# Up projection of a decoder layer on one Trainium2 core: seven block products in place of eight

## The reference, cut to what matters

```python
h = rmsnorm(x, norm_ffn_pre)                  # 512 x 1024
u = h @ w_up                                  # 512 x 5632: 2816 gate and 2816 value columns
u = conv_b + sum(conv_w[j] * shifted(u, j) for j in range(3))    # causal, per column
a, b = split(u, 2)
y = (gelu(a) * b) @ w_down                    # 512 x 1024
x = x + rmsnorm(y, norm_ffn_post)
```

## Time and profile before

| | before |
|---|---|
| median of 3 runs | 630.76 us |
| profiled execution | 631.34 us |
| its span, first to last instruction | 629.5 us |
| PE busy | 619.4 us (98%) |
| DVE busy | 420.6 us (67%) |
| ACT busy | 314.0 us (50%) |
| POOL busy | 98.1 us (16%) |
| mean granted clock of TensorE | 0.998 |

### The profile page before, as it was taken

The page is one execution under the profiler, slowest core; times in us unless marked ns, Lnnn a source line. Parts: engine busy times, 40 slices in busy tenths (PEclk is TensorE's granted clock), DMA queues, the critical chain, the costliest instruction groups (busy, mean ns, idle before and its releaser), DMA issues.

```text
span 629.5 us, 8647 instructions
## 1 busy us (share of the span) xinstructions
PE 619.4 (98%) x3062; PEld 511.7 (81%) x3062; DVE 420.6 (67%) x621; ACT 314.0 (50%) x505; POOL 98.1 (16%) x110
## 2 busy tenths in 40 slices
PE   8999999999999999999999999999999999999996
PEld 7887878778787877899888888888888888888885
DVE  3657449647865876884755556566565668988786
ACT  5557338526735834664533334343333336656661
POOL 4313103112210402420000000000000013532203
PEclk9999999999999999999999999999999999999999
DMA  9834223331512354642433233333323436999923
GB/s 274 239 102 134 67 68 101 100 100 50 150 33 100 121 197 151 199 136 68 133 94 104 74 97 98 100 100 97 103 86 101 166 67 111 188 223 228 232 87 133
DMA packets 91947, 78.90 MB, mean 125 GB/s; under 512 B 2617, under 2 KB 76521, under 8 KB 91922
## 3 DMA queue, kind: packets, MB, share of 16 engines
q1 hardware_dynamic: 84434, 61.79, 32.2%
q0 software_dynamic: 7488, 16.80, 13.2%
HBM read 76.46 MB, written 2.12 MB: 125 GB/s over the span
## 4 chain that ended last, share of the span: by engine, by line
PE 91%; DVE 3%; POOL 2%; DMA 1%; issue 1%; ACT 1%; DVEq 0%; SPq 0%; POOLq 0%; ACTq 0%
PE bank L537 82%; PE bank L679 1%; PE bank L617 1%; DMA gains<-in_norm_mix_pre_dram 1%; PE bank L548 1%; POOL grstd L471 1%; PE bank L668 1%; DVE xs L1326 1%; PE bank L608 1%; PE bank L607 1%; POOL work L475 1%; PE bank L658 1%; PE bank L657 1%; DVE yT L1255 1%; DVE gvar L1295 0%
## 5 line engine op out<-in xcount | busy, mean ns | idle before, releaser
L537 PE MATMUL bank<-hT,ws 128*128 128x512 f32 (+1 forms) x1872 | 410.3, 375 | 0.7 <-DVE work L1304 0.6
L537 PEld LDWEIGHTS bank<-hT,ws 128*128 128x128 f32 x1872 | 328.8, 188 | 61.7 <-issue 2.5
L1208 DVE TENSOR_TENSOR ws<-raw,ws 128x1024 fp32r<-128x1024 f32 x87 | 106.2, 1222 | 7.1 <-ACT ws L894 6.7
L537 PE MATMUL bank<-ws,yT 128*128 128x512 f32 x468 | 109.9, 391 | 0.0
L537 PEld LDWEIGHTS bank<-ws,yT 128*128 128x128 f32 x468 | 87.0, 188 | 18.2 <-issue 0.4
L894 ACT ACTIVATE ws<-raw 128x1024 fp32r<-128x1024 f32 x88 | 92.6, 1054 | 15.6 <-PE bank L537 11.5
L1115 ACT ACTIVATE gains<-bank,conv 128x512 f32<-128x512 f32 x22 | 17.2, 781 | 76.8 <-PE bank L537 76.8
L1470 DVE SCALAR_TENSOR_TENSOR gains<-bank,conv,gains 128x511 f32<-128x511 f32 x22 | 16.5, 750 | 53.8 <-ACT gains L1115 53.8
L520 POOL DMA_DIRECT2D late<-in_w_down_dram x8 | 10.7, 1335 | 253.2 <-DVE ws L1510 253.2
L1115 ACT ACTIVATE rot<-bank,conv 128x512 f32<-128x512 f32 x22 | 17.2, 780 | 63.7 <-PE bank L537 63.7
L537 PE MATMUL bank<-ws,hT 128*128 128x512 f32 x186 | 42.8, 389 | 0.0
(11 more groups left out here) (135 smaller groups left out, 597.4 us busy)
## 6 DMA issues: line engine op xcount, KB each, us to landing
raw<-in_w_up_dram SPq DMA_DIRECT2D x44, 512.0 KB, 3.8
raw<-in_w_in_dram SPq DMA_DIRECT2D x28, 512.0 KB, 4.4
raw<-in_w_out_dram SPq DMA_DIRECT2D x16, 512.0 KB, 3.5
raw<-in_w_down_dram POOLq DMA_DIRECT2D x12, 512.0 KB, 7.7
raw<-in_w_down_dram SPq DMA_DIRECT2D x9, 512.0 KB, 4.0
late<-in_w_down_dram POOLq DMA_DIRECT2D x8, 512.0 KB, 5.9
xs<-in_x_dram SPq DMA_DIRECT2D x6, 512.0 KB, 4.1
late<-in_w_down_dram SPq DMA_DIRECT2D x6, 512.0 KB, 6.9
```

The source lines that it names most:

```text
L537: return nc.tensor.matmul(dst, st, mv, start=start, stop=stop, skip_group_check=onto)
L1208: nc.vector.tensor_tensor(ws[:, c, 1, :], raw[:, c, :], f32(ws[:, c, 0, :]), ALU.subtract).then_inc(w_lo, 1)
```

## The change

Sweeps 0 and 1 stay as they are ("plain"). From sweep 2 on, the two value tiles and two gate tiles of a sweep (256 columns each) by the two halves of D, and the two halves of D by the two halves of the tokens, are a 2x2 by 2x2 block product, computed with seven products of sums of blocks. A product is 2 (tiles of 128 weight columns) x 4 (tiles of D) x 3 matmuls, each with 256 tokens. Products accumulate where they can onto each other in PSUM; the others are copied away by ACT and added by DVE.

- Weights: products 1, 4 and 2 take blocks of w_up as SP loads them. Products 7, 6 and 3 take sums laid on product 1's block one after another by POOL's adding transfers, product 5 one on product 4's. A block is 128 partitions x 4 rows of 256 floats, that is 512 KB in pieces of 1 KB; the down projection's are in pieces of 2 KB, and the old w_up loads were in pieces of 512 bytes.
- Activations: `block_sums` (DVE) makes four sums of blocks of h from a float32 copy that ACT keeps (`h_keep`) and from PSUM; `blocks_hi`, `blocks_lo` split them into `yT`.
- Order: one sweep's seven products lie over 16 places of the unit order, so three sweeps are under way at once. In the steady part the order is 1(i), 3(i-2), 4(i-1), 6(i-1), 2(i), 7(i), 5(i-1). The plain units of sweep 1 stand between the first products, and two down units between the last.
- Results: gate in PSUM banks `x_pair(i)` (three pairs), one product in `y_bank(i)`; the value rows go through `vneg`, which lies over `gains[:, 1]`, so the load of `norm_ffn_post` moves from POOL's queue to SP's, behind the last value tap. The taps of the value columns of block sweeps are stored negated, by three copies in place of one.
- Splits run four units ahead in both loops; PSUM banks and the slots of f's shares are laid out anew, and shares follow `shares_at` in place of a fixed distance of six.

```diff
+UP_WHEN = {1: 0, 2: 4, 7: 5, 4: 9, 6: 10, 5: 13, 3: 15}
+_steady = sorted((7 * (i - PLAIN) + w, (p, i)) for i in range(PLAIN, SWEEP) for p, w in UP_WHEN.items())
...
+_steady += [(at, ("plain", PLAIN - 1, j)) for j, at in enumerate((1, 2, 6, 8))]
+_tail = [(5, SWEEP - 2), (4, SWEEP - 1), (3, SWEEP - 2), (6, SWEEP - 1), ("down", 0), (5, SWEEP - 1), ("down", 1), (3, SWEEP - 1)]
...
+UP_LOADS = {1: (0, 0), 4: (1, 1), 2: (0, 1)}
+UP_ADDS = {7: (1, 0), 6: (1, 1), 3: (0, 1), 5: (1, 0)}
+UP_NEXT = {1: 7, 7: 6, 6: 3, 4: 5}
...
+            for n, unit in enumerate(UP_UNITS):
+                if unit[0] not in UP_NEXT:
+                    continue
+                p, i = UP_NEXT[unit[0]], unit[1]
+                m = UP0 + UP_AT[p, i]
+                pool.wait_ge(raw_loaded[raw_slot_of(m)], 16 * loads_of_slot(m))
+                pool.wait_ge(w_lo, lo_count(UP0 + n))
+                pool.dma_start(up_raw(m).rearrange("p (k n) -> p k n", k=4), up_block(UP_ADDS[p], i),
+                               accum_op=ALU.add).then_inc(raw_added[raw_slot_of(m)], 16)
...
+            def up_product(n):
...
+                pe.wait_ge(w_lo, lo_count(UP0 + n))
...
+                if p == 1 and done < 3:
+
+                    pe.wait_ge(gtap0, (1, 3, 4)[done])
+                    pe.wait_ge(vtap0, (1, 3, 2)[done])
...
+                if p == 4:
+                    pe.wait_ge(p7_kept, done + 1)
+                if p == 5:
+                    pe.wait_ge(v_left, done + 1)
+                if p == 3:
+                    pe.wait_ge(v_right, done + 1)
+                for r in range(2):
...
+                    for k in range(4):
+                        cols = slice(k * 256 + r * P, k * 256 + r * P + P)
+                        for m in range(3):
+                            ins = three(dst, ws[:, c, 0, cols], ws[:, c, 1, cols],
+                                        t_block(p, 0)[:, k, :], t_block(p, 1)[:, k, :], m,
+                                        first and k == 0 and m == 0, k == 3 and m == 2, not first)
...
+            for r in range(2):
+                block_sums(r)
+            AHEAD = 4
+            for n in range(len(UP_UNITS)):
+                up_sum(n)
+                if unit_of(UP0 + n + AHEAD)[0] == "down":
+                    down_lo(unit_of(UP0 + n + AHEAD)[1])
+                else:
+                    up_split_lo(n + AHEAD)
+                up_post(n)
+                if n < 4:
+                    blocks_lo(n)
...
+                if n == AHEAD + EARLY_DOWN:
+                    for r in range(2):
+                        gate_row(SWEEP - 1, r)
+                if n == AHEAD + EARLY_DOWN + 1:
+                    f_tiles(SWEEP - 1)
+                    f_difference(COUPLES - 2)
+                    f_difference(COUPLES - 1)
```

More of the change, by code:

```diff
@@ L394, in _, with plain_block @@
                     load_x(1)
[L395 to L398, removed]
+            def plain_block(i, j):
+                at = j % 2 * DFF + j // 2 * P + i * (2 * P)
+                return w_up_v[:, :, at:at + P]
+            for j in range(4):
+                load(UP0 + j, 0, 0, plain_block(0, j))
             sp.wait_ge(a_scores, 8 * PAIRS)
             sp.wait_ge(r_scores, 8 * PAIRS)
+            for n in range(UP0 + 4, UP0 + len(UP_UNITS)):
+                unit, c = unit_of(n), raw_slot_of(n)
+                if unit[0] == "down" or is_added(n):
+                    continue
+                if before_in_slot(n) is not None:
+                    sp.wait_ge(w_lo, lo_count(before_in_slot(n)))
+                block = plain_block(*unit[1:]) if unit[0] == "plain" else up_block(UP_LOADS[unit[0]], unit[1])
+                sp.dma_start(up_raw(n).rearrange("p (k n) -> p k n", n=block.shape[-1]), block).then_inc(raw_loaded[c], 16)
             for n, (p, g) in enumerate(DOWN_UNITS):
@@ new lines, in c11, with up_sum @@
+            def c11(i):
+                dve.wait_ge(p1_kept, i - PLAIN + 1)
+                here = both(x_pair(i), 0, 256)
+                nc.vector.tensor_tensor(here, here, s1[(i - PLAIN) % 3], ALU.add).then_inc(c11_done, 1)
+            def up_sum(n):
+                p, i = UP_UNITS[n][:2]
+                if p not in (6, 5, 3):
+                    return
+                done = i - PLAIN
+                dve.wait_ge(unit_done, UP0 + n + 1)
+                sums = both(x_pair(i), 256, 512)
+                if p == 6:
+                    dve.wait_ge(p4_kept, done + 1)
+                    if done:
+                        dve.wait_ge(vtap0, 2 * i)
+                    nc.vector.tensor_tensor(vneg[:, :, 0:256], sums, kept4, ALU.add).then_inc(v_left, 1)
+                if p == 5:
+                    dve.wait_ge(p7_kept, done + 1)
+                    nc.vector.tensor_tensor(vneg[:, :, 256:512], sums, kept7[done % 2], ALU.add).then_inc(v_right, 1)
+                if p == 3:
+                    c11(i)
```

479 lines of the change are left out of this document (363 added, 116 removed).

## The result

The changed kernel took 623.14 us (median of 4 runs, 621.97 to 624.81), the kernel before beside it 631.0 (4 runs, 630.18 to 631.71): a ratio of 0.9876, 95% interval 0.9861 to 0.9892. The forecast was 622.0. The profiled execution took 623.34 with a span of 621.5.

The account below looks back on a forecast made before the run. The prediction took TensorE's matmuls to bound the up projection. A gain of 14.4 us less 0.2, 1.0, 3.5 and 0.9 left 8.8, taking the median from 630.76 to 622.0 us, range 615.5 to 636.

Parts of the forecast that it names:

- The gain of 14.4: Up projection: seven products of 2.88 us make a sweep 20.16 us against 21.76, saving 14.4 us over nine sweeps.
- VectorE in the sweeps: Steady sweeps: VectorE has 17.6 us of work in 20.16, 87%, and is not the bound by its sum.
- The tightest wait: Steady sweep: product 3's wait for v_right, needed by 23.04 us and ready at 21.6, slack 1.4 us.
- Transfers: Up projection: an adding 1 KB piece costs 100 ns, DMA 18.1 us per sweep (90%), adds landing in 6.5 to 8.3 us.
- late adds: Sweeps: an occasional adding transfer landing past the 8.9 us there for product 5, charged 0.9 us in all (0 to 13).
- late landing: Rival: adds land past 10.9 us, so TensorE waits before product 3 once per sweep; 627 to 645 us, chance 0.18.
- DMA the bound: Rival: a 1 KB adding piece costs more than 128 ns; midway to 179, 24.9 us per sweep and 664 us; chance 0.14.
- The start: Output projection and BACK: h copies charged 0.2 us, VectorE's queue before product 1(2) 1.0 us (0 to 3).
- The end: From the end of 6(10): VectorE needs 31.0 us, TensorE's units 27.5, so 3.5 us stall at down units 7 and 8.
- about 2 us for ScalarE: The end: VectorE once waits about 2 us for ScalarE, whose two value taps of sweep 10 stand ahead of share 7.
- the rest of the tail is as it was: Down projection after units 7 and 8: nothing charged; two down units moved forward neither add nor save work.
- all is covered: Rival: lags don't meet, so the whole 14.4 us is gained, 616.4 us; chance 0.15.

Follow-up runs that it names:

- Experiment 1: Kernel before, with each up unit of sweeps 1 to 10 run as two halves of 256 tokens, nothing saved: 643.82 us, ratio 1.0200.
- experiment 3: Changed kernel with 18 of the 24 matmuls of product 2 left out in each block sweep: 612.61 us, ratio 0.9707.
- experiment 4: Changed kernel with one more 512 KB memory-to-memory transfer per block sweep, issued by SP: 622.46 us, ratio 0.9865.
- Experiment 6: Changed kernel with the shares for down index 8 and on made later, so fewer stand ahead of g_sums: 622.55 us, ratio 0.9873.
- experiment 12: Changed kernel with VectorE's low parts of the down weights made on 64 of 1,024 columns, waits kept: 616.73 us, ratio 0.9776.
- experiments 5 to 11: Seven variants of the changed kernel that move rows or units near the end, singly or combined, leaving no work out: 621.45 to 626.55 us.
- 7: Changed kernel with unit 6(10) ahead of 3(9) and the rows of both regrouped: 623.60 us, ratio 0.9879.
- 8: Changed kernel with the edits of 5, Experiment 6 and 7 together: 626.55 us, ratio 0.9927.
- 10: Changed kernel with ScalarE making row 7's high part ahead of the last value taps, plus the edit of Experiment 6: 621.45 us, ratio 0.9844.
- 11: 10 plus the last two differences of f on GpSimd, placed further back in its queue than in 5: 621.48 us, ratio 0.9839.
- 5: Changed kernel with the last two differences of f made by GpSimd, ahead of its adding transfer for down index 11: 622.93 us, ratio 0.9869.

## Why the prediction was right, point by point

- **The gain of 14.4.** Right. A sweep takes 20.15 us, and the stretch without VectorE's waits is 334.32 - 320.03 = 14.3 us shorter. Experiment 1 shows the pace by itself. The 2.5 ns of the Trainium skill (TensorE: Matmul & The Clock Gate, "Back-to-back issue gap") stand there for an isolated matmul, and the section says itself that a stream of weight loads and matmuls, which this is, has another spacing; so the prediction and experiment 1's rival priced the wrong case with it. Here the fixed part is 13.3 ns at 256 columns; by 2.5 ns, an estimate, experiment 1's 960 added matmuls would have cost 2.4 us, and they cost 12.7 (643.82 against 631.16 beside it).
- **VectorE in the sweeps.** 17.6 us forecast per sweep; from 341 to 482 us it was busy 119.25 us in seven sweeps, 17.0 each, five shares and differences of f among them, which the 17.6 leaves out. Rows in a full queue start up to 0.1 us before the one ahead has ended (a split of 1.22 us every 1.13), so durations add up to too much. The tightest wait was named right (experiment 3); its slack of 1.4 us is not measured.
- **Transfers.** 100 ns forecast a piece, 104 measured; landing in about 6 us and not the 7 to 9 that were to be a sign of being right; 0.9 us charged for late adds, 0 measured. The two rivals built on them (late landing, DMA the bound; 0.32 together) are excluded: TensorE has no wait in mid stage, and none in experiment 4 either.
- **The start: 0.2 + 1.0 charged, about 0.1 measured.** Behind BACK, product 1(2) comes without a wait that the profile lists; its first starts lie 0.12 us wider than the pace. TensorE and VectorE after:

```profile
290.23 13.95 PE L693 MATMUL bank<-hT,ws 128*128 128x256 f32 x113 [0.15 <-DVE hT L1538]
```
```profile
290.10 0.68 DVE L1890 TENSOR_TENSOR work<-work,bank 128x512 f32<-128x512 f32 x1
...
295.39 1.22 DVE L1816 TENSOR_TENSOR ws<-late,ws 128x1024 fp32r<-128x1024 f32 x1
...
301.01 0.75 DVE L1797 SCALAR_TENSOR_TENSOR gains<-bank,conv,gains 128x510 f32<-128x510 f32 x1
```

  The eight sums took 5.29 us where 8 x 0.69 had been counted, and the last row ended at 301.76; TensorE was through BACK at 290.23 + 11.52 = 301.75. The forecast summed durations; the starts lie closer. That the two met within 0.01 us is luck: the place has no slack. The wait ahead of BACK is the 0.15 of the earlier trace rows still, so the h copies cost nothing.
- **The end: 3.5 charged, 5.6 measured.** Up to unit 8 the sum holds: the loss is 2.55 plus the 0.96 at 5(10), 3.5, and "about 2 us for ScalarE" is the 2.19 of above. VectorE after, at v_left and at unit 8's low part:

```profile
502.35 0.69 DVE L1837 TENSOR_TENSOR gains<-bank,late 128x512 f32<-128x512 f32 x1
...
529.50 1.22 DVE L1930 TENSOR_TENSOR ws<-raw,ws 128x1024 fp32r<-128x1024 f32 x1
```

  From 499.48, where 6(10) ends, to 530.72 are 31.2 us, against 31.0 forecast. But it starts 2.9 us behind there (502.35), not 2.1, and the place 5(10) was not named: with one down unit of 2.75 us between, v_left was late there already. By the forecast's 2.1 it would just have been in time, so this place comes from the lag's size. It is the same debt, paid in two places. What was missing altogether is product 3 of down's first half, 1.65 us: the forecast said that the rest of the tail is as it was. The two operations of g_sums, before and after:

```profile
573.24 1.27 DVE L1530 TENSOR_TENSOR late<-gains,bank 128x512 f32<-128x512 f32 x2
```
```profile
565.25 1.27 DVE L1950 TENSOR_TENSOR late<-gains,bank 128x512 f32<-128x512 f32 x2
```

  Before, they ended at 574.51 and TensorE came for them at 518.79 + 246 x 0.2267 = 574.56, with no slack. After, TensorE would have come at 564.93 and they ended at 566.52: VectorE's queue was still late 35 us behind unit 8. Experiment 6 took 0.75 us of this away by moving three shares behind them, and experiment 12 all of it.
- **The sum.** The stretch gave 14.3 - 5.6 = 8.7; the forecast's 8.8 was 14.4 - 5.6, but of its 5.6 it put 2.1 where next to nothing was lost (the start, the adds) and missed 2.1 at g_sums and in small steps. That these two cancel is luck; the mechanism (fewer matmuls at 120.0 ns, less a debt on VectorE's queue at the end) and the size of 3.5 us were right by themselves. Of the 1.1 us between 622.0 and 623.14, 0.24 is the higher median of before in this comparison (631.0); the rest lies outside the stretch or is spread, for the medians are 7.9 us apart (6.8 to 8.8 by the interval) where the stretch has 8.7.
- **The rival "all is covered"** (616.4) is what experiment 12 comes to, 616.73, with 34 us of VectorE's work left out.

## What to carry to other kernels

When fewer matmuls are bought with more vector work, the steady loop may have room and the joints between stages none: lay out the in-order queue of the helper engine through every joint, up to the next point where a result has no slack, not just to the first wait. Here moving rows about did little for the debt (experiments 5 to 11 gained at most 0.8 us of the stretch's 5.6); taking 34 us of work off the queue removed it (experiment 12). And it pays to measure by a distance within the trace that begins behind the noise: three kernels that should agree did so to 0.04 us (325.65, 325.68, 325.69), where their medians differ by 0.9.

## What the runs showed of the hardware

- **An idle TensorE can lose its clock.** Behind waits of 2.31 us (7 and 8) and 1.81 us (10) it was granted 1.2 GHz for some 3.5 us, which cost 1.5 to 1.6 us more. Behind 1.49 and 1.52 us (the changed kernel), 1.66 (11), 1.71 (5) and once 2.41 us (8, at 568.61) it was not, so the length of the wait alone doesn't tell. Whether this also explains the single slower runs of other kernels (624.81, 624.78 and 624.28 us) stays open: no trace of those was taken, and their mean clock of 0.995 to 0.997 doesn't set them apart (the changed kernel's 621.97 us has 0.997, the fastest run of 7 has 0.994).
- **Adding transfers**: 104 ns for a piece of 1 KB, 179 for one of 2 KB: a straight line through the two gives, as an estimate, some 29 ns a piece and 75 per KB. GpSimd's issue took 1.28 us for 512 pieces, hardly more than the 1.19 for 256, so it isn't priced by pieces alone, as the forecast had it (1.8).
- **DMA at a mean share of 0.99** cost nothing in experiment 4, where an adding transfer landed in 6.6 us and the prediction's layout has 8.9.
